# Down weights of the experts' second column piece, loaded with all 128 partitions written by every transfer

## The reference

```python
def swiglu(h, wg, wu, wd):
    return jnp.einsum('...f,fd->...d', jax.nn.silu(h @ wg) * (h @ wu), wd)

    for e in range(N_EXPERTS):
        out = out + dense_gate[:, e:e + 1] * swiglu(ht, wg[e], wu[e], wd[e])
```

## Time and profile before

| | |
|---|---|
| median of 3 runs | 1458.16 us (1456.94 to 1464.88) |
| profiled execution | 1463.24 us, span 1461.4 us |
| mean granted TensorE clock | 0.986 |
| TensorE busy | 1385.4 us (95%) |
| ScalarE, VectorE busy | 384.2 us (26%), 514.8 us (35%) |
| read from and written to device memory | 396.78 MB and 16.12 MB, 283 GB/s over the span |
| share of the 16 DMA engines' span taken by SyncE's queue (q1) | 75.0% |

### The profile page before, as it was taken

The page is one execution under the profiler, slowest core; times in us unless marked ns, Lnnn a source line. Parts: engine busy times, 40 slices in busy tenths (PEclk is TensorE's granted clock), DMA queues, the critical chain, the costliest instruction groups (busy, mean ns, idle before and its releaser), DMA issues.

```text
span 1461.4 us, 32936 instructions
## 1 busy us (share of the span) xinstructions
PE 1385.4 (95%) x14972; PEld 960.7 (66%) x14972; DVE 514.8 (35%) x836; ACT 384.2 (26%) x527; POOL 75.0 (5%) x130
## 2 busy tenths in 40 slices
PE   7999999999999999999989989989979969999998
PEld 6879998897845655754453453543534549788896
DVE  6975555389531001010010000100101164657665
ACT  5664443346400000000000000000000045656653
POOL 3400000033010000000000000000001010000000
PEclk9999999999899999999999999999999989999999
DMA  9569864454879999999999999999999945243341
GB/s 321 163 223 327 295 227 173 144 174 155 315 296 365 379 390 336 415 376 336 407 314 372 382 288 413 375 321 407 327 381 377 319 165 179 96 144 116 116 174 58
DMA packets 122571, 407.12 MB, mean 279 GB/s; under 512 B 7430, under 2 KB 35958, under 8 KB 122436
## 3 DMA queue, kind: packets, MB, share of 16 engines
q1 hardware_dynamic: 114192, 389.57, 75.0%
q0 software_dynamic: 5408, 12.58, 2.6%
q10 hardware_dynamic: 2836, 2.88, 0.6%
HBM read 396.78 MB, written 16.12 MB: 283 GB/s over the span
## 4 chain that ended last, share of the span: by engine, by line
PE 61%; DMA 21%; DVE 7%; SPq 7%; issue 2%; ACT 2%; ACTq 0%; DVEq 0%; POOL 0%; POOLq 0%
PE ps L2701 24%; DMA ering<-in_moe_wu 8%; PE ps L516 6%; PE ps L518 6%; SPq L452 6%; PE ps L517 6%; DMA ering<-in_moe_wd 5%; DMA ering<-in_moe_wg 4%; DVE yT L2027 3%; DMA ys<-eo 2%; PE ps L1198 2%; PE ps L1200 2%; PE ps L1199 2%; DVE low L506 1%; DMA rawb<-in_w_in 1%
## 5 line engine op out<-in xcount | busy, mean ns | idle before, releaser
L2701 PE MATMUL ps<-ering,xe 128*32 128x384 f32 (+1 forms) x6144 | 464.1, 461 | 13.2 <-issue 5.1
L2701 PEld LDWEIGHTS ps<-ering,xe 128*32 128x32 f32 x6144 | 213.4, 110 | 258.4 <-issue 126.2
L2701 PE MATMUL ps<-ering,eT 128*32 128x256 f32 x4224 | 240.9, 385 | 25.9 <-DMA ering<-in_moe_wd 22.4
L2701 PEld LDWEIGHTS ps<-ering,eT 128*32 128x32 f32 x4224 | 147.0, 111 | 116.7 <-issue 21.6
L2203 DVE TENSOR_TENSOR eh<-eh,ps 128x384 f32<-128x384 f32 (+1 forms) x48 | 22.1, 516 | 558.9 <-PE ps L2701 558.9
L506 DVE TENSOR_TENSOR low<-raw,high 128x2048 fp32r<-128x2048 f32 (+3 forms) x48 | 128.8, 2685 | 61.6 <-ACT high L501 60.4
L501 ACT ACTIVATE high<-raw 128x2048 fp32r<-128x2048 f32 (+3 forms) x47 | 105.5, 2244 | 91.8 <-PE ps L518 76.2
L516 PE MATMUL ps<-high,xT_hi 128*128 128x352 f32 (+1 forms) x368 | 128.3, 349 | 1.2 <-DVE xT_lo L2109 1.2
L518 PE MATMUL ps<-high,xT_lo 128*128 128x352 f32 (+1 forms) x368 | 127.1, 346 | 0.0
L517 PE MATMUL ps<-low,xT_hi 128*128 128x352 f32 (+1 forms) x368 | 126.8, 345 | 0.0
L1880 ACT ACTIVATE eh<-ps 128x384 f32<-128x384 f32 (+1 forms) x48 | 18.8, 464 | 365.5 <-PE ps L2701 365.5
(11 more groups left out here) (436 smaller groups left out, 1670.6 us busy)
## 6 DMA issues: line engine op xcount, KB each, us to landing
ering<-in_moe_wg SPq DMA_DIRECT2D x32, 1536.0 KB, 26.3
ering<-in_moe_wu SPq DMA_DIRECT2D x32, 1536.0 KB, 28.4
ering<-in_moe_wd SPq DMA_DIRECT2D x32, 1536.0 KB, 21.9
ering<-in_moe_wg SPq DMA_DIRECT2D x32, 1280.0 KB, 23.5
ering<-in_moe_wu SPq DMA_DIRECT2D x32, 1280.0 KB, 21.8
rawb<-in_w_in SPq DMA_DIRECT2D x25, 1024.0 KB, 5.1
ering<-in_moe_wd SPq DMA_DIRECT2D x24, 1024.0 KB, 20.5
raw<-in_w_in SPq DMA_DIRECT2D x16, 1024.0 KB, 8.9
```

Of the source, the lines that this page charges most:

```text
L2701: mm = nc.tensor.matmul(out_of(rows), tokens, weights[:, n * s:n * s + n], start=begins, stop=ends, skip_group_check=True)
```

## The change

Chunks 20, 21 and 23 are loaded differently. Before, chunk 20 holds tiles 12, 13 and 14, in a transfer of two tiles and one of a single tile, because tile 14 lies in the next strip; chunk 21 holds tiles 15, 16 and 17, in one of a single tile and one of two. After, chunk 20 holds tiles 12, 14 and 16 (the first full tile of strips 0, 1 and 2) and chunk 21 tiles 13, 15 and 17, each in one transfer. Chunk 23 is the rests: before, two transfers that each write 64 partitions of both tiles; after, two that each write all 128 partitions of one tile, the upper and the lower 64 from two places of the weights. `LANDINGS` and `DOWN_TILES` follow.

```diff
-    LANDINGS = [2 if j in (20, 21, 23) else 1 for j in range(FFN_CHUNKS)]
-    DOWN_TILES = ((0, 1, 2), (3, 4, 5), (6, 7, 8), (9, 10, 11), (12, 13, 14), (15, 16, 17), (18, 19), (20, 21))
+    LANDINGS = [2 if j == 23 else 1 for j in range(FFN_CHUNKS)]
+    DOWN_TILES = ((0, 1, 2), (3, 4, 5), (6, 7, 8), (9, 10, 11), (12, 14, 16), (13, 15, 17), (18, 19), (20, 21))
...
-        elif j == 20:
-            tiles(0, strip(0), 2)
-            tiles(2, strip(1), 1)
-        elif j == 21:
-            tiles(0, strip(1) + P, 1)
-            tiles(1, strip(2), 2)
+        elif j < 22:
+            jb = j - 20
+            source = wd_v[e, PIECE0:, :].rearrange("(s q) n -> q s n", s=STRIPS)[jb * P:jb * P + P, 0:3, :]
+            rows(slot_view(ering, s, 3, D), source)
         elif j == 22:
-            tiles(0, strip(3), 2)
+            tiles(0, PIECE0 + 3 * WIDE[1], 2)
         else:
-            ends = wd_v[e, PIECE0:, :].rearrange("(t u q) n -> u q t n", t=2, u=2)
-            for u in range(2):
-                rows(slot_view(ering, s, 2, D)[2 * STRIP * u:2 * STRIP * u + REST, :, :], ends[u, 2 * P:, :, :])
+            ends = wd_v[e, PIECE0:, :].rearrange("(t u q) n -> t u q n", t=2, u=2)
+            for t in range(2):
+                rows(slot_view(ering, s, 2, D)[:, t, :], ends[t, :, 2 * P:, :])
```

More of the change, by code:

```diff
@@ L456, in tiles @@
                  wd_v[e, first:first + count * P, :].rearrange("(t p) n -> p t n", p=P))
-        def strip(n):
-            return PIECE0 + WIDE[1] * n
         if j < 16:
```

## The result

The changed kernel takes 1614.13 us (median of 4 runs, 1612.81 to 1615.47) against 1459.52 us for the kernel before in the same comparison: ratio 1.105, 95% interval 1.102 to 1.109. It is slower by 155 us; 1656 was forecast, in a range of 1535 to 1730.

What follows compares the result with a forecast made beforehand. DMA was taken to bound the later items, 99.3 us each against TensorE's 89.9. Item 0's chunk 23 at 511.6, plus seven items of 123.6, less 6 at the end, gave +198: 1656 us, range 1535 to 1730.

Steps and rivals of the forecast that it cites:

- The bound now: In the experts' stage, later items are bound by DMA at 99.3 us each, against TensorE's own pace of 89.9.
- Half speed comes from partitions that engines share: Transfers to 64 or 96 partitions put two engines on one group; slow stretches took 10.2 us an item.
- Chunks 20 and 21 at nothing: Loading these down weights with two issues fewer costs 0; under 2 x 0.7 us an item gained if SyncE were late.
- The new chunk 23 on two engines: Its source's outermost count of 2 limits each transfer to two engines, which set the pace from item 1.
- Rival 3: All 16 engines carry the new chunk 23, as the cap might look at the target alone: 1416 us, chance 0.10.
- X: Time chunk 23's new transfers take on the two engines in each item: 34 us, between 20.3 free and 40.6 doubled.
- Items 1 to 7: Two engines need 86.6 us of other work, 3 for the tokens and 34 for chunk 23: 123.6 us an item.
- The end: The second block's first weights are issued earlier, shortening the chain's 18.49 us wait for them: 6 us off.
- Rival 1: Two engines carry chunk 23 free of contention, 20.3 us, giving 108.9 us an item: 1540 us, chance 0.18.
- rival 2: Two engines carry chunk 23 doubled throughout, 40.6 us, giving 132.2 us an item: 1723 us, chance 0.17.
- the main case: Two engines carry chunk 23 with part of the contention, giving 123.6 us an item: 1656 us, chance 0.53.
- TensorE's clock: Idle some 30 us before each chunk 23, TensorE may run at a lower clock, hidden behind the next wait.

Runs made afterwards that it cites:

- old23: The changed kernel with chunk 23 loaded as before, in two transfers to 64 partitions, chunks 20 and 21 staying in one transfer each: 1458.8 us, ratio 0.999.
- run128: The changed kernel with each of chunk 23's two sources one run of 128 consecutive rows (wrong rows, same bytes and targets): 1408.5 us, ratio 0.965.
- plain: The kernel before with strips 1 and 3 shifted 64 columns, so all down weights come in transfers of 128 consecutive rows: 1406.9 us, ratio 0.965.
- plain128: The kernel with plain rows of down weights, and the next tokens loaded as 128 rows in place of 96: 1402.9 us, ratio 0.963.
- cap16: The changed kernel with chunk 23's source taken from sixteen blocks of 8 rows (wrong rows, same bytes and targets): 1450.4 us, ratio 0.992.
- only23: The kernel before with only chunk 23 loaded in the new way: 1611.8 us (1 run).
- after128: The changed kernel with the next tokens loaded as 128 rows in place of 96: 1607.8 us, ratio 1.102.
- one23: The changed kernel without the second of chunk 23's two transfers: 1520.4 us (1 run).
- cap8: The changed kernel with chunk 23's source taken from eight blocks of 16 rows (wrong rows, same bytes and targets): 1483.9 us, ratio 1.016.

## Why the prediction was right, and where its size was off

**The bound now:** right. Change chunk 23's source and target alone (`old23` to `run128`) and items go from 99.9 to 88.5 us, where TensorE no longer waits for weights; `plain`, another layout, has the same 88.5. The floor that I read as 89.9 is 88.5; the early items of the kernel before already held small waits.

**Half speed comes from partitions that engines share:** borne out in effect. `run128` against `old23` changes only chunk 23's pattern and rows, and the dips at the item's end and 50 us go; `plain128` against `plain` removes the tokens' dip. But "all 128 partitions" was too coarse, in the change and in my reading: `cap16` writes all 128 on 16 engines and keeps most of the loss. Laying the earlier dip to the tokens was right, too (2.4 us of DMA time in `plain`); keeping 3 us of it in the changed kernel was too much.

**Chunks 20 and 21 at nothing:** right (`old23`, 0.997 to 1.002; `only23`).

**The new chunk 23 on two engines:** right, and shown by the two-engine rate of 52 GB/s and by its growth to 109 and 207 with four and eight blocks. Reading the cap from the stores of `ys`, a pattern that was not to be changed, carried the forecast. Rival 3, all 16 engines, fell: the cap looks at the source too. (Its 98.5 us an item stands in no row; the earlier trace rows give 99.3. Its 1416 for 16 engines is bracketed by `cap16`, 1450.4, and `run128`, 1408.5.)

**The size:** forecast +198 on the profiled execution, measured 1611.0 - 1461.4 = +149.6. Four terms, by my own sum:
- Item 0's chunk 23 was put at 511.6; it was there at 501.0: -10.6. There the stretch with two engines alone was short (57 GB/s from 475 to 480), and then 253 to 281 GB/s moved until 500; why it came sooner than put was not taken apart.
- Items 1 to 7 were put at 123.6 us; they took 117.5: 7 x 6.1 = -43. Of these 6.1 some 2 to 2.5 are the 3 us kept for the tokens (`after128` gives 0.5 to 1). The rest, some 4 us, is X: 34 was forecast, and 117.5 - 86.6 - 0.5 to 1 leaves about 30.
- The end was put at -6; the rest of the difference, 151.2 at chunk 23 of item 7 against 149.6 in the span, makes it -1.6: +4.4. The 6 us were for second-block weights that are issued earlier. They were not: the chain waits 17.63 us for them in place of 18.49, and they land at 1332.13, 8.7 us behind the start of item 7's chunk 23, as before (1180.96 and 1172.27).

The sum is -49, the gap. X was too large in how I split it: I let the other engines be busy for 27 us beside the two and both sides go at half speed throughout. The windows show them idle for 17 us ahead (from 815), starting only about 832, and then all 16 moving 275 and soon 361 to 389 GB/s, over the 207 of a fully doubled stretch. That fits the 189 ns of the second 64 packets (`one23`); the 290 ns of the first 64 show that a contended stretch comes already with one such transfer. How the contended part depends on the order in which the two engines go through the partitions is left open. That the two engines' full queues hold SyncE up is read from its 12.7 us for one transfer and from the idle engines; no experiment removed it alone. Of the other signs named, TensorE idled 23 us for 30, and the landing time of the 512 KB transfers can't be read.

**Rival 1** (no contention, 1540) and **rival 2** (doubled throughout, 1723) bracket the result, 74 us above the one and 109 below the other; the truth was between the main case and rival 1.

**TensorE's clock** fell to 0.50 in the waits and made the 48 matmuls behind them 5.35 us for 2.80. As forecast it stays hidden, since an item of 117.5 us needs only 88.5 of TensorE, except once at the end of the stage (the last chunk's 48 matmuls, 4.09 us for 2.80).

## What to carry to other kernels

Look at both sides of a transfer: the outermost count of the source caps the engines (2, 4 and 8 here) as the target's does (the stores of `ys`, by the prediction's estimate), so a target of 128 partitions filled from two blocks of rows is carried by two engines. A DMA share near n/16 with GB/s near n times one engine's rate is how it looks in a trace, and a row of issues without a landing time is a weak hint of it. A share of 1 at little over half the GB/s is the other fault, by the reading above engines that write into each other's partitions. What cured both here was a layout in which each transfer is a run of 128 rows. Moving the accumulator's columns by 64 bought it for no matmul more (14972 in both), with two more copies an item on VectorE, and one multiply and one activation fewer.

## What the runs showed of the hardware beyond that

- Sixteen blocks of 8 rows and 32 blocks of 4 rows, the same bytes to the same 128 partitions on 16 engines, differ by 42 us in the whole (1450.4 and 1407.9), that is by 9.2 us in an item for 1 MB of its 34.6 MB.
- Eight engines on chunk 23 (`cap8`) give the item that the kernel before has with 16 engines on 64 partitions each (99.9 and 100.2 us, items 3 to 6), though the whole takes 25 us more: it falls back by 12 us between items 0 and 3 and by 9 between items 6 and 7.
- The loss reaches far beyond the transfers that cause it: 1 MB an item, 2.5 us at full rate, cost the kernel before at least 11.7 us an item (100.2 against 88.5). That engines already on other chunks meet those writes is my reading of it; the traces don't show which engine waits.
